# A state-space stage whose causal mask moves out of TensorE: ScalarE clips the exponents, VectorE masks the table of input products

## The reference, cut to what matters

```python
adt = (dt * a)                              # never positive: dt > 0, a < 0
a_cs = jnp.cumsum(adt, axis=-1)
seg = a_cs[..., :, None] - a_cs[..., None, :]
lmat = jnp.exp(jnp.where(causal, seg, -jnp.inf))
cb = jnp.einsum('bclgn,bcsgn->bcgls', cc, bc)
y_diag = jnp.einsum('bcgels,bcsgep->bclgep', cb[:, :, :, None] * lmat, xdt)
...                                         # states between chunks, y_off
gated = rms_norm(y * silu(z), 1.0)
```

## Time and profile before

| | |
|---|---|
| median of 3 runs | 2188.64 us (2188.14 to 2189.06) |
| the profiled execution | 2191.19 us, span of the core 2189.5 us |
| mean granted TensorE clock | 0.981 |
| busy in the span | TensorE 2099.9 us, VectorE 1539.3, ScalarE 915.2, GpSimd 402.1 |
| the stage of the change | first instruction at 1471.65 us, last norm matmul at 1584.25 us |

### The profile page before, as it was taken

How to read it: one execution, slowest core, us unless ns; L and a number is a source line. 1 busy time by engine, 2 the same in 40 slices (tenths; PEclk the granted TensorE clock), 3 DMA queues, 4 the chain that set the end, 5 groups by cost and what they waited for, 6 DMA issues and landing times. The chain is left out here.

```text
span 2189.5 us, 27551 instructions
## 1 busy us (share of the span) xinstructions
PE 2099.9 (96%) x10453; PEld 1627.0 (74%) x10453; DVE 1539.3 (70%) x2228; ACT 915.2 (42%) x1573; POOL 402.1 (18%) x300
## 2 busy tenths in 40 slices
PE   6999997879999999999999999999999999999999
PEld 4778753567778888887887778986768977543887
DVE  4899769586898777776658885218856288575894
ACT  3454122543652333335446542336544333345343
POOL 0000000312334365650000100014200000265000
PEclk8999998979999999999999999999999999999999
DMA  8556038105524466659764321100231210101933
GB/s 287 169 179 219 4 93 336 63 20 168 173 84 151 136 208 214 207 182 299 249 201 139 94 64 50 30 1 20 68 92 52 65 39 20 78 11 45 269 116 97
DMA packets 298940, 273.19 MB, mean 125 GB/s; under 512 B 21395, under 2 KB 242379, under 8 KB 298009
## 3 DMA queue, kind: packets, MB, share of 16 engines
q1 hardware_dynamic: 273244, 247.96, 35.7%
q10 hardware_dynamic: 22284, 11.16, 1.8%
q0 software_dynamic: 3280, 12.32, 1.5%
HBM read 208.29 MB, written 61.92 MB: 123 GB/s over the span
## 5 line engine op out<-in xcount | busy, mean ns | idle before, releaser
L2723 PE MATMUL bk_in<-t_part,a 128*128 128x512 f32 x1272 | 296.2, 391 | 2.7 <-DVE arena L3178 2.1
L2723 PEld LDWEIGHTS bk_in<-t_part,a 128*128 128x128 f32 x1272 | 239.6, 189 | 54.7 <-issue 4.3
L2753 PE MATMUL bk_in<-hid_part,o_part 128*128 128x512 f32 x792 | 182.0, 391 | 0.1
L2753 PEld LDWEIGHTS bk_in<-hid_part,o_part 128*128 128x128 f32 x792 | 148.6, 188 | 32.6 <-issue 1.4
L1131 PE MATMUL fr_ps<-fr_h,fw 128*128 128x512 f32 x576 | 137.2, 399 | 0.8 <-ACT fr_h L1382 0.7
L2723 PE MATMUL ml_o<-t_part,a 128*128 128x512 f32 x576 | 135.2, 389 | 0.3 <-ACT arena L2809 0.3
L1131 PEld LDWEIGHTS fr_ps<-fr_h,fw 128*128 128x128 f32 x576 | 108.6, 190 | 27.3 <-issue 1.2
L2796 ACT ACTIVATE a<-s_raw 128x512 fp32r<-128x512 f32 x88 | 55.6, 632 | 167.9 <-PE bk_in L2723 92.7
L2723 PEld LDWEIGHTS ml_o<-t_part,a 128*128 128x128 f32 x576 | 108.0, 188 | 23.1 <-issue 0.7
L3551 PE MATMUL bk_in<-h_part,sj_part 128*128 128x512 f32 x456 | 105.0, 391 | 1.4 <-DVE sj_part L3513 1.4
L4143 PE MATMUL ss_a<-h_part,aj_part 128*128 128x512 f32 x432 | 105.8, 400 | 0.0
(11 more groups left out here) (777 smaller groups left out, 4464.7 us busy)
## 6 DMA issues: line engine op xcount, KB each, us to landing
work<-in_w_mod SPq DMA_DIRECT2D x20, 1024.0 KB, 7.5
hid_raw<-kept_hid SPq DMA_DIRECT2D x35, 512.0 KB, 5.6
work<-in_w_in SPq DMA_DIRECT2D x27, 512.0 KB, 3.8
g_raw<-in_w_ffn_in SPq DMA_DIRECT2D x24, 512.0 KB, 4.4
arena<-in_w_ffn_out SPq DMA_DIRECT2D x22, 512.0 KB, 4.9
kept_s<-arena SPq DMA_DIRECT2D x22, 512.0 KB, 4.4
w_raw<-kept_s SPq DMA_DIRECT2D x16, 704.0 KB, 4.3
work<-in_w_in ACTq DMA_DIRECT2D x21, 512.0 KB, 3.8
```

What stands on the lines that cost most here:

```text
L2723: mm = pe.matmul(bank, ring[n % 4][a][:, k, :], moving[:, b, k, :], start=(opens and k == 0 and j == 0), stop=(k == HK - 1 and j == 2), sk ...
L2753: mm = pe.matmul(bank, o_part[u % 2][:, a, k * P:(k + 1) * P], tile_at(j, k)[:, b, :], start=(opens and k == 0 and i == 0), stop=(k == PAI ...
```

## The change

TensorE no longer adds the mask: the second matmul of each quarter is gone. ScalarE reads each quarter twice. First comes a Relu of the negated exponent, from PSUM into `E`; it makes every exponent above the diagonal, which would be positive, zero. Then an Exp of the negated result works in place in SBUF. The quarters go in pairs: two Relus, then two Exps. A bank `pa` is now free after its Relu. VectorE multiplies the two tables `cb` in `pg` by the 0/1 mask `t_le` ahead of the products, in place in PSUM (128x256). The two operations that laid out identity and mask for TensorE are gone.

```diff
@@ SsdProjection.vector @@
-        nc.vector.tensor_copy(S.ss_ident[:, :], S.ident)
-        nc.vector.tensor_scalar(S.ss_early[:, :], S.t_le, -1.0, 1e30, ALU.add, ALU.mult)
@@ stage_ssd @@
+        clipped = lambda c, q: 8 * c + 4 * (q // 2) + q % 2 + 1
...
-                    takes(seg_bank, 4 * c + q, s.E, 4 * c + q + 1)
+                    takes(seg_bank, 4 * c + q, s.E, clipped(c, q))
@@ tensor, decays @@
                         if c:
-                            pe.matmul(pa[:, bank % 3, :], lead[c % 2][rows, :],
-                                      trail[c % 2][rows, :, :].rearrange("p h l -> p (h l)"), start=True, stop=False)
+                            mm = pe.matmul(pa[:, bank % 3, :], lead[c % 2][rows, :],
+                                           trail[c % 2][rows, :, :].rearrange("p h l -> p (h l)"), start=True, stop=True)
...
-                        pe.matmul(pa[:, bank % 3, :].rearrange("p (h l) -> p h l", l=P), ident_r[:, :],
-                                  early_r[:, :].unsqueeze(1).broadcast_to([P, 4, P]), start=False, stop=True)\
-                            .then_inc(s.seg, 1)
...
+                        mm.then_inc(s.seg, 1)
@@ scalar, decays @@
-                    for q in range(4):
-                        u = 4 * c + q
-                        act.wait_ge(s.seg, u + 1)
-                        if c >= 2:
-                            act.wait_ge(s.Y, c - 1)
-                        nc.scalar.activation(E[c % 2][:, 4 * q:4 * q + 4, :],
-                                             pa[:, seg_bank[u] % 3, :].rearrange("p (h l) -> p h l", l=P), ACT.Exp)\
-                            .then_inc(s.E, 1)
+                    for pair in ((0, 1), (2, 3)):
+                        for q in pair:
+                            u = 4 * c + q
+                            act.wait_ge(s.seg, u + 1)
+                            if c >= 2:
+                                act.wait_ge(s.Y, c - 1)
+                            nc.scalar.activation(E[c % 2][:, 4 * q:4 * q + 4, :],
+                                                 pa[:, seg_bank[u] % 3, :].rearrange("p (h l) -> p h l", l=P), ACT.Relu,
+                                                 scale=-1.0).then_inc(s.E, 1)
+                        for q in pair:
+                            act.wait_ge(s.E, clipped(c, q))
+                            e = E[c % 2][:, 4 * q:4 * q + 4, :]
+                            nc.scalar.activation(e, e, ACT.Exp, scale=-1.0).then_inc(s.E, 1)
@@ vector, products @@
                     dve.wait_ge(s.G, c + 1)
+                    both = pg[:, 0:SSD_G * P].rearrange("p (g l) -> p g l", l=P)
+                    nc.vector.tensor_tensor(both, both, S.t_le.unsqueeze(1).broadcast_to([P, SSD_G, P]), ALU.mult)\
+                        .then_inc(s.laid, 1)
+                    dve.wait_ge(s.laid, c + 2)
                     for g in range(SSD_G):
-                        dve.wait_ge(s.E, 4 * c + 2 * g + 2)
+                        dve.wait_ge(s.E, 8 * c + 4 * g + 4)
```

More of the change, by code:

```diff
@@ L3454, in __init__ @@
                       5: rounded(nc, S, "sj_sixth", XC0 + 8 * T, 2, T)}
-        S.ss_ident = rounded(nc, S, "ss_ident", YY0 + 2048, P)
-        S.ss_early = rounded(nc, S, "ss_early", YY0 + 2048 + 128, P)
         self.R = A.view(XC0 + 4 * T, SSD_H, P)
@@ L4675, in stage_ssd @@
     at = YY0 + 2048
-    ident_r, early_r = S.ss_ident, S.ss_early
     diag = A.view(at + 256, 2, P)
@@ L4691, in stage_ssd @@
         S.ssd_sent = semaphores(nc, S, S.past_ssd, "sz", "sent")
-        s = semaphores(nc, S, ctx, "ss", "consts cum parts skip xdt xds G seg E M offs decayed added Y summed y_ok kept st_mm"
+        s = semaphores(nc, S, ctx, "ss", "laid cum parts skip xdt xds G seg E M offs decayed added Y summed y_ok kept st_mm"
                                       " upd sq ms root inv diag turned outa outd")
@@ L4762, in decays @@
                         if c:
-                            pe.matmul(pa[:, bank % 3, :], lead[c % 2][rows, :],
-                                      trail[c % 2][rows, :, :].rearrange("p h l -> p (h l)"), start=True, stop=False)
-                        else:
-                            pe.matmul(pa[:, bank % 3, :], S.t_gt, R[:, 4 * q:4 * q + 4, :].rearrange("p h l -> p (h l)"),
-                                      start=True, stop=False)
-                        pe.matmul(pa[:, bank % 3, :].rearrange("p (h l) -> p h l", l=P), ident_r[:, :],
-                                  early_r[:, :].unsqueeze(1).broadcast_to([P, 4, P]), start=False, stop=True)\
-                            .then_inc(s.seg, 1)
+                            mm = pe.matmul(pa[:, bank % 3, :], lead[c % 2][rows, :],
+                                           trail[c % 2][rows, :, :].rearrange("p h l -> p (h l)"), start=True, stop=True)
+                        else:
+                            mm = pe.matmul(pa[:, bank % 3, :], S.t_gt,
+                                           R[:, 4 * q:4 * q + 4, :].rearrange("p h l -> p (h l)"), start=True, stop=True)
+                        mm.then_inc(s.seg, 1)
                 def turn(c):
@@ L4822, in lru_products @@
                                       stop=(k == KT - 1 and a == 1), skip_group_check=True)
-                pe.wait_ge(s.E, 4 * NC)
+                pe.wait_ge(s.E, 8 * NC)
                 pe.wait_ge(v.hi, 1)
@@ L4896, in _ @@
             def _(dve):
-                nc.vector.memset(eps, EPS).then_inc(s.consts, 1)
+                nc.vector.memset(eps, EPS).then_inc(s.laid, 1)
                 def products(c):
                     dve.wait_ge(s.G, c + 1)
+                    both = pg[:, 0:SSD_G * P].rearrange("p (g l) -> p g l", l=P)
+                    nc.vector.tensor_tensor(both, both, S.t_le.unsqueeze(1).broadcast_to([P, SSD_G, P]), ALU.mult)\
+                        .then_inc(s.laid, 1)
+                    dve.wait_ge(s.laid, c + 2)
                     for g in range(SSD_G):
-                        dve.wait_ge(s.E, 4 * c + 2 * g + 2)
+                        dve.wait_ge(s.E, 8 * c + 4 * g + 4)
                         e = E[c % 2][:, g * HG:(g + 1) * HG, :]
@@ L4926, in mean @@
                     if c == 0:
-                        dve.wait_ge(s.consts, 1)
+                        dve.wait_ge(s.laid, 1)
                     nc.vector.scalar_tensor_tensor(out=ms[:, c, :], in0=ms[:, c, :], scalar=1.0 / HALF, in1=eps,
```

## The result

The changed kernel takes 2214.40 us (2212.39 to 2216.5), the kernel before beside it 2188.85 (2188.14 to 2190.79): 1.0108 times, 95% interval 1.009 to 1.0126. The forecast was 2196.2 with a range of 2187 to 2203. The direction was right, the size was missed by 18 us, and the range did not hold the time.

A forecast was written before the change was run, and what follows sets the result against it. TensorE's queue was taken to set the pace, 12.77 us a chunk, with ScalarE's ring at 12.43. Stretches of -0.3, +1.0, +3.3, 0 and +2.0 gave +6.0, with one slow stretch +7.6: 2196.2 us, range 2187 to 2203.

The forecast's parts named there:

- The ring through ScalarE: Exponent matmuls, Relus and Exps, Squares, `out`, `Y`, next exponents: 14.43 us a turn after, against TensorE's 12.77 before.
- The load: Exp table load on ScalarE falls between second Relu and first Exp, no longer hidden: 1.40 us in five chunks.
- VectorE's mask: Eight mask operations on VectorE, nearest row 0.422 us, ahead of its wait for the Exps: costed at nothing.
- The tail: Chunk 7 to the end, where VectorE is the chain: +2.0 us.
- The clock: TensorE's granted clock: one slow stretch of 1.62 us counted again, raising +6.0 to +7.6 us.
- Slow clock in each turn: Rival, chance 0.08: with TensorE idle ahead of `Y`, each of five turns loses 1.62 us, giving 2202.7 us.
- The head: Stage up to chunk 4: chunk 3's exponents about 0.7 us earlier, one turn adds 1.66, together +1.0 us.

The follow-up runs named there:

- keep_busy: Changed kernel with thirteen identity matmuls, results unused, ahead of `Y` in chunks 3 to 6: 2201.64 us, ratio 1.0052.
- busy_load_early: keep_busy with 6 fillers instead of 13, 8 and 12 more in iterations 0 and 1, and a tiny Exp ahead of chunks 3 to 7's Relus: 2195.11 us.
- table_mask_alone: Kernel before with only VectorE's mask on the two tables added, mask matmuls kept: 2188.93 us, ratio 1.0001.
- keep_half: keep_busy with 6 identity matmuls instead of 13 ahead of `Y`: 2215.34 us, ratio 1.0112.
- scalar_alone: Kernel before with only ScalarE's Relu and Exp in pairs; TensorE still adds the masks: 2221.19 us, ratio 1.014.
- load_early: Changed kernel with one tiny unused Exp ahead of the Relus of chunks 3 to 7: 2200.43 us, ratio 1.0045.
- grouped_mean: Kernel before with mask matmuls grouped three and one, and `mean` on one SBUF input and two constants: 2184.55 us, ratio 0.9969.

## Why the prediction was wrong

- *The ring through ScalarE.* Right. 14.43 forecast, 14.32 to 14.33 in keep_busy; the gap ahead of `Y` about 3 forecast, 2.95 measured; its releaser is `out`. In the changed kernel the low clock lengthens it to 17.65 to 18.91.
- *The load.* Right: 1.40 forecast, 1.43 by busy_load_early against the 14.33 of keep_busy, and no second load for Relu.
- *VectorE's mask.* Right, free by table_mask_alone.
- *The tail.* Right at full clock: +2.0 forecast, 43.48 - 41.53 = +1.95 in keep_busy. The changed kernel's +3.07 is 1.1 more.
- *The clock.* The step that failed is "The stretch of the earlier trace rows cost 14.39 - 12.77 = 1.62; ... so I count one again", and with it the rival "Slow clock in each turn", given 0.08 and priced at 1.62 a turn. The clock fell in each turn, as that rival says, and its price is 17.65 - 14.33 = 3.3, 18.91 - 14.33 = 4.6 and 17.96 - 14.33 = 3.6, together 11.5 us. 1.62 was taken from a turn where the clock was low without a gap before it, and for little more than the 16 norm matmuls (3.53 us; 1.95 at the upper clock). In the ring after, the low clock begins behind the gap and covers `Y` and the state matmul, 5.6 us of work that all lies on the ring and takes up to 9.9. The rival at 3.8 a turn would have given 6.0 + 5 x 3.8 = 25 us; that this is near the 25.6 between the medians is partly luck, since in the trace the clock's share is 14.6 us and not 19. The argument against it, that other chunks kept the full clock, came from chunks without a gap and said nothing about a ring with one.
- *The head.* +1.0 forecast, +4.85 measured. From chunk 3 to 4 it is 16.31 us where the ring at full clock is 14.33; the 2.0 between are about what the low clock added to `turn(0)` (3.78 - 1.95 = 1.8) and to the state's part behind it (2.34 - 1.88 = 0.5), an estimate that no run isolates. The wait ahead of `turn(0)` was not foreseen: the prediction let GpSimd's products hold up only `mean`, and they fell on two more operations. Ahead of chunk 3 it is +1.3, which the forecast had at about -0.7, because the state matmul was to start as soon as `Y` was done. Instead it waited 1.39 us more for `added` (L4949): VectorE came straight from chunk 2's last product by the table, which had waited for ScalarE's Exp and starts 24.7 us into the stage instead of 21.3. Earlier on TensorE waits 1.81 and 0.60 us for ScalarE and VectorE, and `Y(0)` takes 4.95 us at the low clock. How this part divides was not tried.

Taken together, at full clock the change costs -1.04 + 2.9 (head without the 2.0) + 3.1 + 1.95 = 6.9 us, against 6.0 forecast; the clock adds 2.0 + 11.5 + 1.1 = 14.6. That is the 21.48 of the table, to rounding. The 6.9 is closer to 6.0 than its parts are: without the -1.04, which cannot be told from scatter, it is 7.9, and the excess lies in the head.

## What to carry to other kernels

When a change turns a dense TensorE into one that waits once per iteration, price the work behind that wait at the lower clock as well as the wait itself; here each 3 us of idle time in the steady turns cost 3 to 5 us more. With shorter gaps it went both ways, so there it belongs in the range. Before taking work off an engine, ask which ring of releases closes when it is gone, and whether the same saving is to be had by order alone: grouping the masks kept ScalarE's work as it was and won 0.35%.

## What the runs showed of the hardware

- A gap of 2.95 us in a turn brought the granted clock to the lower level for about 7 us in each turn. So did 1.57 us in keep_half and 2.13 us in scalar_alone, while 1.53 to 1.64 us in load_early did so twice in four, and single gaps of 1.65 us (before) and 1.95 us (keep_busy) near the stage's end did not. Filling the gap with useless matmuls won some 12 us.
- Three matmuls that read 32 rows each, from different rows, take 0.50 us together, and one alone takes 0.50. Alternating with matmuls of 128 rows, one starts every 0.43. From the first of the six matmuls to the end of the last it is 1513.31 - 1511.92 = 1.39 us in groups, where six alternating ones took 1516.26 + 0.50 - 1514.12 = 2.64. The Trainium skill says that a change of tiling mode drains TensorE (TensorEngine Tiling (Array Packing), Key Properties). The runs agree with it, but they do not separate a drain from the overlap that the 32-row matmuls lose when a 128-row one stands between them.
- A GpSimd product of 128x1024 held up VectorE's operations with SBUF operands: 2.52 instead of 1.22 us and 2.00 instead of 0.49, both gone when the products were cut to one head. An operation with one input in SBUF was held up as well (1.37 us beside GpSimd in grouped_mean, 0.16 otherwise).
